# Prompt queries of latent attention: the rotary rows of four heads in one tile, rotated by VectorE, and the other rows copied by ScalarE

## What is computed

```python
def mla_project(h, pos, w_dq, q_norm, w_uq, w_dkv, kv_norm, w_uk):
    cq = rms_norm(h @ w_dq, q_norm)                       # 512 wide
    q = (cq @ w_uq).reshape(B, T, N_HEADS, QK_NOPE + QK_ROPE)   # 16 heads, 64 + 32
    q_rope = rope(q[..., QK_NOPE:], pos)
    q_lat = jnp.einsum('bthn,khn->bthk', q[..., :QK_NOPE], w_uk)
    kv = h @ w_dkv
    ckv = rms_norm(kv[..., :KV_LORA], kv_norm)            # 256 wide
    kr = rope(kv[..., KV_LORA:], pos)                     # 32 wide, one for all heads
def rope(x, pos):
    x1, x2 = x[..., :16], x[..., 16:]
    return concatenate([x1 * cos - x2 * sin, x2 * cos + x1 * sin])
```

## Time and profile before

| | |
|---|---|
| median of 3 runs | 2587.83 us (2586.87 to 2588.07) |
| the profiled execution, its own time | 2589.02 us |
| its span in the profile | 2587.2 us |
| TensorE busy | 2455.6 us, 95% |
| VectorE busy | 1702.3 us, 66% |
| ScalarE busy | 1279.1 us, 49% |
| mean granted clock of TensorE | 0.983 |

### The profile page before, as it was taken

How to read it: one execution, slowest core, us unless ns; L and a number is a source line. 1 busy time by engine, 2 the same in 40 slices (tenths; PEclk the granted TensorE clock), 3 DMA queues, 4 the chain that set the end, 5 groups by cost and what they waited for, 6 DMA issues and landing times.

```text
span 2587.2 us, 48510 instructions
## 1 busy us (share of the span) xinstructions
PE 2455.6 (95%) x18652; PEld 2254.9 (87%) x18652; DVE 1702.3 (66%) x3278; ACT 1279.1 (49%) x2916; POOL 314.2 (12%) x341
## 2 busy tenths in 40 slices
PE   7989999999889899999999999999999999999996
PEld 5866766665669889999999999999989999999996
DVE  4545555556223677766678867777785877866666
ACT  5634444444125665444465555555645555544444
POOL 0000000000002331000023113103222401200003
PEclk9999999999899999999999999999999999999998
DMA  7022222226434122222232222223222222232221
GB/s 268 13 95 94 94 94 94 94 83 245 161 112 169 58 82 82 91 82 90 90 102 83 78 71 86 82 83 119 87 75 76 91 82 91 83 125 90 91 90 66
DMA packets 71732, 255.07 MB, mean 99 GB/s; under 512 B 7858, under 2 KB 15410, under 8 KB 64594
## 3 DMA queue, kind: packets, MB, share of 16 engines
q1 hardware_dynamic: 71074, 251.83, 28.6%
q10 hardware_dynamic: 432, 0.15, 0.0%
HBM read 244.88 MB, written 7.07 MB: 97 GB/s over the span
## 4 chain that ended last, share of the span: by engine, by line
PE 52%; DVE 10%; ACT 3%; issue 3%; POOL 2%; DMA 0%; POOLq 0%; ACTq 0%; DVEq 0%
PE psum L2553 10%; PE psum L2552 10%; PE psum L2551 10%; PE psum L2526 5%; PE psum L2528 5%; PE psum L2527 5%; DVE t_conv L2383 3%; DVE t_w_lo L2365 2%; DVE t_y L2415 1%; PE psum L2506 1%; PE psum L2504 1%; PE psum L2505 1%; PE psum L2079 1%; POOL t_stat L2005 1%; DVE t_scaled L1846 1%
## 5 line engine op out<-in xcount | busy, mean ns | idle before, releaser
L2551 PE MATMUL psum<-t_h,t_w_hi 128*128 128x272 f32 x2816 | 816.4, 290 | 3.2 <-DVE t_w_lo L2365 3.2
L2553 PE MATMUL psum<-t_h,t_w_lo 128*128 128x272 f32 x2816 | 812.9, 289 | 0.0
L2552 PE MATMUL psum<-t_h,t_w_hi 128*128 128x272 f32 x2816 | 811.8, 288 | 0.0
L2551 PEld LDWEIGHTS psum<-t_h,t_w_hi 128*128 128x128 f32 x2816 | 531.3, 189 | 4.6 <-DVE t_w_lo L2365 3.4
L2552 PEld LDWEIGHTS psum<-t_h,t_w_hi 128*128 128x128 f32 x2816 | 531.7, 189 | 1.1
L2553 PEld LDWEIGHTS psum<-t_h,t_w_lo 128*128 128x128 f32 x2816 | 531.6, 189 | 0.0
L2383 DVE SCALAR_TENSOR_TENSOR t_conv<-t_u,t_taps,t_conv 128x272 f32<-128x272 f32 (+2 forms) x528 | 339.9, 644 | 152.3 <-ACT t_conv L2287 146.1
L2526 PE MATMUL psum<-t_g_hi,t_w_hi 128*128 128x272 f32 x1408 | 409.9, 291 | 26.6 <-DVE t_w_lo L2365 16.5
L2415 DVE TENSOR_TENSOR t_y<-psum,t_y 128x272 f32<-128x272 f32 x640 | 279.8, 438 | 199.9 <-PE psum L2528 195.7
L2527 PE MATMUL psum<-t_g_lo,t_w_hi 128*128 128x272 f32 x1408 | 405.0, 288 | 0.0
L2528 PE MATMUL psum<-t_g_hi,t_w_lo 128*128 128x272 f32 x1408 | 404.5, 287 | 0.0
(11 more groups left out here) (211 smaller groups left out, 3520.8 us busy)
## 6 DMA issues: line engine op xcount, KB each, us to landing
t_raw<-in_ffn_w SPq DMA_DIRECT2D x264, 512.0 KB, 3.4
late_w<-in_ada_late SPq DMA_DIRECT2D x40, 1024.0 KB, 4.8
cache<-in_cache SPq DMA_DIRECT2D x64, 320.0 KB, 4.8
t_raw<-in_wo SPq DMA_DIRECT2D x16, 512.0 KB, 3.4
ada_w<-in_ada_w SPq DMA_DIRECT2D x6, 1024.0 KB, 7.5
x<-in_x SPq DMA_DIRECT2D x2, 2176.0 KB, 10.9
proj_raw<-in_proj_w SPq DMA_DIRECT2D x8, 448.0 KB, 5.0
out_x_out<-x SPq DMA_DIRECT2D x3, 1088.0 KB, 7.3
```

The source lines that it names most:

```text
L2551: pe.matmul(bank, t.w_hi[s][:, o], hi, start=kt == 0, stop=False)
L2552: pe.matmul(bank, t.w_hi[s][:, o], lo, start=False, stop=False)
L2553: last = pe.matmul(bank, t.w_lo[s][:, o], hi, start=False, stop=kt == KT - 1)
```

## The change

The queries of the prompt are laid out anew:

- A plain job `("n", c)` makes the 64 plain rows of both heads of the pair for chunk c. ScalarE evacuates it with two copies of 64 partitions, and for the last chunk with two more of the 64 sample columns.
- A rotary job `("r", c)` makes the 32 rotary rows of the four heads of two pairs, in bands of 32 partitions. It is made for even pairs only. VectorE evacuates it in `turn_rope` with a multiply by the cosines over 128 partitions and four multiplies by the sines of 32 partitions each, from the neighbouring band. In the next slot `add_rope` adds the two: three sums, one of them into `next_rope` for the odd pair, and for the last chunk four more for the sample columns.
- In an odd pair's slots two copies of 64 x 1024 (`place_next_rope`) bring `next_rope` into `q`, and three slots have no product.
- The weights of odd pairs are 1024 columns and their split 512 wide.
- Each band of 32 partitions holds 16 rotary rows twice, so the shared rotary key is laid out to suit: `turn_keys` ends with two scalings by a column of ones and zeros in place of the copy, the cached rotary keys are laid out so in the inputs, and `kr_out` leaves in two DMAs.

```diff
-        Q_JOBS = [("q", hh, c) for hh in range(2) for c in range(NC)]
-        JOBS = [("k", 0), ("k", 1), ("v", 0), *Q_JOBS[0:2], ("v", 1), *Q_JOBS[2:]]
+        KV_FIRST = [("k", 0), ("k", 1), ("v", 0)]
+        SLOTS = [[*KV_FIRST, ("n", 0), ("r", 0), ("v", 1), ("n", 1), ("r", 1), ("n", 2), ("r", 2)],
+                 [*KV_FIRST, ("n", 0), ("place", 0), ("v", 1), ("n", 1), ("place", 1), ("n", 2), None]]
...
-                dve.wait_ge(rot, 4 * c + 3)
-                dve.tensor_copy(m.kr[0:64, cols], m.kr[64:P, cols]).then_inc(rot, 1)
+                dve.wait_ge(rot, 5 * c + 3)
+                for half, part in ((slice(0, 64), LT + QT + 1), (slice(64, P), LT + QT)):
+                    dve.tensor_scalar(m.kr[half, cols], m.kr[64:P, cols], gain[64:P, part:part + 1], None, ALU.mult)\
+                       .then_inc(rot, 1)
...
-            sp.dma_start(io["kr_out"], m.kr[0:ROPE, :]).then_inc(latent_out, 16)
+            for half in range(2):
+                sp.dma_start(io["kr_out"][half * ROPE // 2:(half + 1) * ROPE // 2], m.kr[64 + 32 * half:80 + 32 * half, :])\
+                  .then_inc(latent_out, 16)
...
+        def split_w(i):
+            return QT * P if i % 2 else 2 * QT * P
...
             (ScalarE, job)
+                else:
+                    t0, w = prompt_cols(half)
+                    for hh in range(2):
+                        r = slice(64 * hh, 64 * hh + 64)
+                        if half == NC - 1:
+                            act.activation(m.qs[r, 2 * i + hh, :], bank[r, w:w + NS], ACT.Copy, scale=SCALE)
+                        last = act.activation(q[s][r, hh, t0:t0 + w], bank[r, 0:w], ACT.Copy, scale=SCALE)
...
             (VectorE)
-                dve.tensor_tensor(q[s][:, hh, t0:t0 + w], bank[:, 0:w], rot[:, hh, t0:t0 + w], ALU.mult)\
-                   .then_inc(job_d, 1)
+            def turn_rope(i, c):
+                ...
+                dve.tensor_tensor(by_cos[:, 0:w], bank[:, 0:w], rot[:, 0, t0:t0 + w], ALU.mult)
+                for to in range(4):
+                    at = to ^ 1
+                    dst, src = slice(32 * to, 32 * to + 32), slice(32 * at, 32 * at + 32)
+                    last = dve.tensor_tensor(by_sin[dst, 0:w], bank[src, 0:w], rot[src, 1, t0:t0 + w], ALU.mult)
+                    if to < 3:
+                        last.then_inc(by_table, 1)
+                last.then_inc(job_d, 1)
+            def add_rope(i, c, s):
+                ...
+                if c == NC - 1:
+                    for h in range(4):
+                        to = slice(0, 64) if h % 2 else slice(64, P)
+                        dve.tensor_tensor(m.qs[to, 2 * i + h, :], *both(h // 2, slice(w, w + NS)), ALU.add)
+                dve.tensor_tensor(next_rope[64:P, t0:t0 + w], *both(1, slice(0, w)), ALU.add)
+                dve.tensor_tensor(q[s][64:P, 0, t0:t0 + w], *both(0, slice(0, w)), ALU.add)
+                dve.tensor_tensor(q[s][0:64, 1, t0:t0 + w], *both(0, slice(0, w)), ALU.add).then_inc(roped, 1)
+            def place_next_rope(i, hh, s):
+                dve.wait_ge(roped, ROPE_JOBS * (i // 2 + 1))
+                to = slice(0, 64) if hh else slice(64, P)
+                dve.tensor_copy(q[s][to, hh, :], next_rope[64:P, :]).then_inc(rope_placed, 1)
+            def job(i, n, s):
+                before, now = slot(i, n - 1), slot(i, n)
+                if before and before[0] == "r":
+                    add_rope(i, before[1], s)
+                if now and now[0] == "r":
+                    turn_rope(i, now[1])
+                if now and now[0] == "place":
+                    place_next_rope(i, now[1], s)
```

More of the change, by code:

```diff
@@ L169 @@
 PAIR_W = 2 * QT * P + 2 * LT * P
+ODD_W = PAIR_W - QT * P
+KV_W = 2 * LT * P
 CACHE_W = KV_LORA + LT * PAGE + PAGE
@@ L739, in mla_prompt_stage, with slot, jobs, jobs_before @@
         block = own.enter_context(nc.Block())
-        Q_JOBS = [("q", hh, c) for hh in range(2) for c in range(NC)]
-        JOBS = [("k", 0), ("k", 1), ("v", 0), *Q_JOBS[0:2], ("v", 1), *Q_JOBS[2:]]
[L745 to L748, removed]
+        KV_FIRST = [("k", 0), ("k", 1), ("v", 0)]
+        SLOTS = [[*KV_FIRST, ("n", 0), ("r", 0), ("v", 1), ("n", 1), ("r", 1), ("n", 2), ("r", 2)],
+                 [*KV_FIRST, ("n", 0), ("place", 0), ("v", 1), ("n", 1), ("place", 1), ("n", 2), None]]
+        FIRST_Q = len(KV_FIRST)
+        ROPE_JOBS = NC
+        def slot(i, n):
+            return SLOTS[i % 2][n] if 0 <= n < len(SLOTS[0]) else None
+        def jobs(i):
+            return [x for x in SLOTS[i % 2] if x and x[0] != "place"]
+        def jobs_before(i):
+            return sum(len(jobs(p)) for p in range(i))
         n_blocks = lambda n: n // 2 + 1
@@ L842, in job_counts @@
         def job_counts(i, job):
-            return (sum(BY_DVE) * i + sum(BY_DVE[:job]), sum(BY_ACT) * i + sum(BY_ACT[:job]))
+            made = [x for p in range(i) for x in jobs(p)]
+            made += jobs(i)[:job] if job else []
+            by_dve = sum(kind == "r" for kind, _ in made)
+            return by_dve, len(made) - by_dve
+        def split_w(i):
+            return QT * P if i % 2 else 2 * QT * P
         @block.scalar
@@ L852, in split, with job @@
                 act.wait_ge(raw_in[s], n - 16 * (1 - s))
[L853 to L857, removed]
+                act.wait_ge(job_done, jobs_before(i))
+                act.activation(wq_hi[:, 0:split_w(i)], raw[s][:, KV_W:KV_W + split_w(i)], ACT.Copy).then_inc(wq_hi_ready, 1)
+            def job(i, what, s):
+                if not what or what[0] in ("r", "place"):
                     return
-                kind, half = JOBS[j]
+                kind, half = what
+                j = jobs(i).index(what)
                 bank = bank_of_job(i, j)
-                act.wait_ge(job_done, 10 * i + j + 1)
+                act.wait_ge(job_done, jobs_before(i) + j + 1)
                 if kind == "k":
@@ L901, in pair @@
                         split(i + 2, s, 16 * (i // 2 + 2))
[L902 to L907, removed]
+                    if not last:
+                        job(i + 1, slot(i + 1, n), 1 - s)
+            act.activation(wq_hi[:], raw[0][:, KV_W:PAIR_W], ACT.Copy).then_inc(wq_hi_ready, 1)
+            for what in SLOTS[0]:
+                job(0, what, 0)
             exps(0, 0, 0)
@@ L1003, in pair @@
                         split(i + 2, s)
-                    if n in SLOT_OF_JOB and not last:
-                        job(i + 1, SLOT_OF_JOB[n], 1 - s)
+                    if not last:
+                        job(i + 1, n, 1 - s)
             split(0, 0)
-            for j in range(len(JOBS)):
-                job(0, j, 0)
+            for n in range(len(SLOTS[0]) + 1):
+                job(0, n, 0)
             place_rope(1)
@@ L1050, in job @@
                 else:
-                    half = JOBS[j][1]
                     for b in range(4):
@@ L1135, in pair @@
                         score(*at(i, n, 2), s if n + 2 < STEPS else 1 - s)
-                    if n in SLOT_OF_JOB and not last:
-                        job(i + 1, SLOT_OF_JOB[n], 1 - s)
+                    if not last and slot(i + 1, n) in jobs(i + 1):
+                        job(i + 1, jobs(i + 1).index(slot(i + 1, n)), 1 - s)
                     turn_late(whole_group(jj, b, n - 1))
@@ L1146, in pair @@
                     late_products(late(jj, b, n), late_group(jj, b, n))
-            for j in range(len(JOBS)):
+            for j in range(len(jobs(0))):
                 job(0, j, 0)
@@ L2611, in swapped, with twice, by_tile @@
     return np.concatenate([w[..., ROPE // 2:], w[..., :ROPE // 2]], axis=-1)
+def twice(v, axis=-1):
+    return np.concatenate([np.concatenate([h, h], axis=axis) for h in np.split(v, 2, axis=axis)], axis=axis)
+def by_tile(w):
+    return w.reshape(QT, P, -1, P).transpose(2, 1, 0, 3).reshape(-1, P, QT * P)
 def attention_inputs(a):
```

95 lines of the change are left out of this document (54 added, 41 removed).

## The result

| | before | after |
|---|---|---|
| median of 20 runs each | 2588.19 us | 2592.47 us |
| lowest to highest | 2583.80 to 2591.46 | 2587.90 to 2596.45 |
| the profiled execution, its own time | 2589.02 | 2596.45 |
| its span | 2587.2 | 2594.7 |
| mean granted clock | 0.983 | 0.979 |

The ratio is 1.0016, with a 95% interval of 1.0010 to 1.0023. The change costs about 4.3 us, inside the 0.2% that the prediction called the same and inside its range, but on the slow side and resolved from none. The profiled execution of after was the longest of its 20, so the two profiles lie 7.5 us apart where the medians lie 4.3 apart.

The account below looks back on a forecast made before the run. TensorE bounds the kernel (busy 95%) while job-bank evacuations stay shorter than its work between jobs; -23.6 + 15.0 + 6.9 - 0.7 + 0.45 + 2 = +0.05 gave about 2587.9 us as a median, range 2579 to 2596.

Parts of the forecast that it names:

- odd preparation: Jobs for pairs 1, 3, 5, 7: rotary query jobs removed in steps 4, 7, 9; -5.9 us each, four -23.6.
- splits: Weight splits of odd pairs halve: 0.2 us less at three, nearly nothing at the first, -0.7 in all.
- even preparation: Jobs for pairs 2, 4, 6: TensorE waits for ScalarE copies and VectorE rotations; 5.0 us each, three +15.0.
- first pair: Jobs before pair 0's first scores: two waits of 1.3 us, then 4.3 at the end; together +6.9 us.
- key rotation's tail: Last chunk's key rotation ends with two scalings in place of a 0.32 us copy: +0.45 us at the stage's end.
- clock: Granted clock may fall after TensorE's stands in step 10 and before the first scores: +2 us (0 to 8.5).
- Pair 7 as a yardstick: Steps 3 to 10 take 16.14 us without jobs, 27.42 with; a removed job is given back almost whole.
- fourth rival: ScalarE's query copies delay exponentials in steps 4, 7, 9; odd preparations give 3, not 5.9; 2599.6 us, chance 0.06.
- first rival: Band multiplies overlap like full-height work and the clock holds: -8.5 us, 2579.4 us, chance 0.17.
- second rival: Multiplies of 32 partitions cost half those of 64, a rotation 1.8 us: -13 us, 2575 us, chance 0.05.
- sums behind step 9: In even preparations add_rope delays VectorE's normalising of step 11: 0 to 2.3 us per pair, taken as 0.
- third rival: Three step 10 waits and two in the first pair bring clock falls, 8.5 us for 2; 2594.4 us, chance 0.12.

Follow-up runs that it names:

- products in the stand: Twelve unused products of 384 columns before the values product of step 10 in pairs 1, 3 and 5, against the changed kernel; 2587.66 us, 1.0000 to before.
- products before the first scores: Thirty unused products of 384 columns in TensorE's stand ahead of pair 0's first scores, against the changed kernel; 2593.59 us, one run.
- plain rows by VectorE: Plain query jobs of odd pairs copied by VectorE in place of ScalarE, against the changed kernel; 2600.21 us, one run.
- all multiplies in one band: The four sine multiplies all read and write partitions 0 to 31, without band exchange, against the changed kernel; 2584.93 us, one run.
- Staged and moved: ScalarE copies the rotary bank to SBUF, VectorE rotates later; pair 0's key placing earlier, last rotation later; against the changed kernel; 2565.15 us, 0.9919 to before.

## Why the prediction held, and where it was off

The direction and the size of nearly every step held. Each is set against what the profiles gave:

| step | forecast | measured |
|---|---|---|
| odd preparation, each of four | -5.9, and -0.2 of splits | -5.9 in pairs 2, 4, 6, splits included |
| a rotation of 384 columns | 2.9 | 2.88 |
| even preparation, each of three, clock aside | +5.0 | +5.4 |
| first pair, to the first scores | +6.9 | +6.8 |
| key rotation's tail | +0.45 | two scalings of 0.81 us in all for a copy of 0.32 |
| clock | +2 | +5.6 |

**Odd preparations.** The time came out of the steps named: step 4 by 1.6 us (a job of 2.09, less the 0.5 for ScalarE's copies), steps 6 and 7 together by 1.8, step 9 by 1.8, and step 10 by 0.5, where VectorE's queue no longer holds two rotations. Pair 7 as a yardstick was sound, and the fourth rival, that the freed time isn't given back, fell.

**Even preparations.** In steps 4, 5, 6 to 8, and 10 with 11 the prediction had 0.3, 1.2, 1.5 and 2.0 us. The runs gave 0.3, 1.4, 1.6 and, with the products in the stand, 2.2. The pitch of 0.58 decided between the forecast and the first rival, and one multiply in place of four showed that these waits come from the rotation. The second rival, cheaper multiplies on 32 partitions, fell by the same rows. The sums behind step 9, the narrowest place of the argument, cost nothing.

**The clock** is the term that was mis-sized. Three falls of 1.5 us, as the products in the stand showed, are 4.6. In pair 0 the low clock costs 2.5 us, but the kernel before had a fall there too: its pair 0 took 63.86 us, and 56.53 + 5.9 = 62.4 is what it would be at the full clock, so about 1.4 (an estimate). That leaves 1.0, and 5.6 in all, where the prediction had 2. The prediction let the 2.70 us stand without a fall weigh as much as the 2.07 us with one, and took +2 in place of what the third rival said. That rival was right in its mechanism for the three stands of step 10, and too high in its price (8.5) by taking 1.7 us for a fall, counting two for the first pair and nothing for the one that was there before. The Trainium skill, TensorE: Matmul & The Clock Gate, section HAM oscillation, describes a kernel in which waits of about 3 to 5 us part short bursts of matmuls, and the clock falls back at every one. The stands of step 10 are shorter, and the traces agree in part: the fall came behind all three stands of after and of the kernel with products before the first scores (2.88 us), two of three with plain rows by VectorE (2.88) and two of three with all multiplies in one band (2.28). What decides it isn't shown here; each of these kernels was profiled once.

The sum in measured terms: 4 x -5.9 + 3 x 5.4 + 6.8 + 0.45 + 5.6 = +5.5 us, for 4.3 between the medians with an interval of 2.6 to 6.0 (0.10 and 0.23% of 2588). With the forecast's +2 for the clock and 5.0 for an even preparation it had been +0.7. So 3.6 of the difference is the clock and 1.2 the three even preparations; the remaining 0.6 is mostly the splits of odd pairs, which the forecast counted beside the -5.9 and the measured -5.9 contains.

The agreement in the whole is close to the edge: 4.3 us lies under the 5.2 that the prediction called the same, but the interval reaches 6.0. Its statement that less than 0.2% can't be told from none was too careful, as 20 runs of each told 0.16%. Two of its side sums don't come out as written: with the second rival's waits the terms add up to -13.7 us and not -13, and with the short pitch the first pair comes to 5.7 us and not 5.2 (two waits of 0.9 and 3.9 at its end, with the sums left at 2.3). Neither bears on the forecast.

So the change exchanges time for time. It takes 24 us of products away, and gives it back because four short multiplies hold the only job bank for 2.9 us, stand ahead of the mask in VectorE's queue in step 10, and stand ahead of the keys in pair 0. Staged and moved, the same idea is worth 0.8%.

## What to carry to other kernels

What counts of an evacuation is how long it holds its bank and what stands behind it in its engine's queue, not its busy time: here three rotations of up to 2.9 us cost 5.4 to 6.9 us a pair, and in the pairs nothing once a copy of 0.49 us by an engine with room had freed the bank and the rotations stood a slot later. Before splitting one instruction by bands of partitions, price it as that many full instructions. Where a change makes TensorE stand for 2 us and more, charge the stand and a likely clock fall behind it, 1.5 us here, and look whether the stand can be moved behind other work first.

## What the runs showed of the hardware that was not expected

- A stand of 2.88 us in step 10 was followed by about 3.4 us at 1.2 GHz in eight of nine cases in three kernels, one of 2.28 us in two of three; twelve products of 384 columns (2.57 us) put into the stand kept the clock at 2.4 GHz and delayed nothing.
- A multiply of 32 x 384 takes 0.53 to 0.56 us, about as long as one of 128 x 384 (0.56). Started in the same band as the one before, it follows after 0.47 us; in another band, after 0.58.
- A plain copy of 128 x 384 out of PSUM took ScalarE 0.49 us, and the same 0.49 for half the partitions (0.98 for two of 64 x 384).
